# Modulation blocks in the even projection's weight stream: fewer among the attention's levels, more among the last blocks

## The chip, the cores and the metric

The kernel runs on one core of one Trainium2 chip. The metric is the device time of one execution in microseconds, lower is better. Before the change three runs gave 1708.02, 1708.63 and 1709.81 us, median 1708.63.

## What is computed

A two-layer hybrid block is followed by a second hybrid layer. Only the first mixer of the first block matters here. Two vectors of conditions (one for the context, one for the latents) are put through a silu and multiplied with a 1024 x 6144 matrix `mod_w` for each layer; the 48 groups of 128 results are shifts, scales and gates. The 512 tokens (256 context, 256 latent) are normalised and modulated with the first 16 groups. They are then projected, and the projected features feed a gated linear attention and an mLSTM:

```
def modulate(x, g, shift, scale):
    return rmsnorm(x, g) * (1 + scale) + shift

gq, gk, gv, gg, mq, mk, mv, mo, mg = _split(h @ w_in, EVEN_SIZES)
log_a = log_sigmoid((h @ a1[d]) @ a2[d] + ab[d]) / GLA_TAU
qk = silu(dwconv1d(concatenate([mq, mk]), conv_w, conv_b))
```

In `gla_scan` the scores need `exp(cum[t] - cum[s])` inside a chunk.

## The kernel before, in words

All weights lie in DRAM as blocks of 128 x 1024 floats (eight 128 x 128 tiles, 512 KB), in the order of the list `STREAM` (line 115). SP loads them one after another into a ring of four slots (`load_weights`, line 278). The load at place p of the stream waits until the block at place p - 4 is released, and since SP takes them in order, a load also waits for all loads ahead of it.

Two kinds of blocks share this stream in the even projection:

- 31 product blocks `even_in`. ScalarE (ACT) makes the rounded high part (line 375). For blocks 3 to 7 VectorE (DVE) makes the low part (line 385). From block 8 on ACT writes the negated high part (line 378), and a DMA of POOL adds the weights from DRAM to it (line 392). Such a block's slot is free when its high part is made. TensorE (PE) multiplies three passes (high by high, high by low, low by high).
- 28 modulation blocks `mod0` 16 to 43. DVE handles one with two multiply-and-accumulate instructions, one for each vector of conditions (line 865), and its slot is free after the second. Their sums are read in later stages.

`run_products` (line 402) writes every engine's program, item by item (item e is one 128-feature output of all tokens, or one tile of tokens; each is 24 passes of TensorE). Four banks hold the items. `low_parts` places the modulation blocks in DVE's order: before DVE goes past product block n it handles every modulation block that stands ahead of n in `STREAM`. At item e the bound is `due[e]`, here block e + 3. Within the last convolution (items 17 and 18) DVE is asked to go one block further, to block 22, between two taps:

```
ahead = parts_due(first + last_of[convs[-1]]) + AHEAD
...
if t == n_taps // 2 and group[-1] == len(convs) - 1:
    low_parts(ahead)
```

Items 0 to 4 are features (`low`, `gq`, `gk`), 5 to 8 token tiles (`gv`), 9 and 10 gates, 11 to 18 go through a convolution (two taps on DVE, line 706, in pairs of items), 19 to 22 are `mv`, 23 to 26 `gg`, 27 to 30 `mo`.

Beside the items runs `GlaSteps`, the gated linear attention, placed by half items ("ticks", two to an item). Its seven levels begin at tick 13 and are four ticks apart. For each level DVE subtracts sums (line 1832), ACT takes exponentials (line 1756), DVE takes the scores of the level before (line 1807) and makes four products (lines 1846 to 1849), and PE computes the scores (line 1634, 32 matmuls). So DVE's turn of the levels 5, 6 and 7 lies in items 14 and 15, 16 and 17, 18 and 19. After the levels come the keys (line 1870, items 22 and 23), the states (lines 1881 and 1884, items 24 to 26), and among them the mLSTM's gates: DVE sums and scans them in items 24 and 25 (lines 1950 to 1971), ACT makes `floors` (line 1975), and PE turns them (lines 1981 and 1982) in item 26, in front of that item's second half. The next round (`mo`) needs all four banks.

Each engine takes its instructions in the written order, so what DVE is given ahead of a level delays that level.

Of the kernel before, what the change touches and what calls it, by code (L numbers as in the profile page):

```python
# [56 lines left out]
TOGETHER = 3  # L57
# [22 lines left out]
def blocks_of(name):  # L80
    first = FIRST_TILE[name] // TPB
    return list(range(first, first + N_TILES[name] // TPB))
# [9 lines left out]
def spread_among(few, many):  # L92

    out, placed = [], 0
    for i, b in enumerate(many):
        while placed < len(few) * (i + 1) // len(many):
            out.append(few[placed])
            placed += 1
        out.append(b)
    return out  # L100


MOD_FIRST = 16
MOD_GROUP = 4
MOD_STRIP = 32
SQUARES_AT = 6
MOD_EVEN = 44
MOD_DOWN = 27
MOD_ODD = 42
DOWN_FIRST = 4  # L110
# [2 lines left out]
SSD_ENTERING = 4  # L113

STREAM = blocks_of("mod0")[:MOD_FIRST] + blocks_of("even_in")[:TOGETHER] \
    + spread_among(blocks_of("mod0")[MOD_FIRST:MOD_EVEN], blocks_of("even_in")[TOGETHER:]) \
    + blocks_of("even_out")[:TOGETHER] + spread_among(blocks_of("mod0")[MOD_EVEN:], blocks_of("even_out")[TOGETHER:]) \
    + blocks_of("up0") + blocks_of("down0")[:DOWN_FIRST] \
    + spread_among(blocks_of("mod1")[:MOD_DOWN], blocks_of("down0")[DOWN_FIRST:]) \
    + blocks_of("ssd_in")[:TOGETHER] + spread_among(blocks_of("mod1")[MOD_DOWN:MOD_ODD], blocks_of("ssd_in")[TOGETHER:MOD_SSD]) \  # L120
    + blocks_of("ssd_in")[MOD_SSD:]
# [237 lines left out]
def run_products(K, rounds, mods=None, prepare=None, beside=None, banks=BANKS, acc_slots=8, fill=0, tail=0):  # L359

    with K.scope():
        _run_products(K, rounds, mods, prepare, beside or Beside(), banks, acc_slots, fill, tail)
# [29 lines left out]
def first_together(rounds, n=TOGETHER):  # L396


    return [[it for r in rounds[:n] for it in r]] + rounds[n:]
# [1040 lines left out]
def even_mixer(K, f, gates, modulator):  # L1440

    ending = MlstmEnding(K, f, gates[2])
    with K.scope():
        mlstm(K, f, *gates, ending)

    with K.activations(KD * T):
        parts = ending.of([(f[name][:, j, :], *K.h_parts(T, base + j))
                           for name, base in (("gg", 0), ("mq", 4)) for j in range(4)])
        run_products(K, first_together(residual_items(K, "even_out", KD, lambda k: K.h_parts(T, k), 0,
                                                      lambda m, which: K.mod[:, 0, 16 + m, which:which + 1])),  # L1450
                     (modulator, blocks_of("mod0")[MOD_EVEN:]), prepare=parts, beside=SumSquares(K, 0), banks=BANKS - 1,
                     fill=8)
# [11 lines left out]
def even_projection(K, f, normalise, modulator, a2, gate_buffers):  # L1464
# [11 lines left out]
    def put(dest, func, scale=1.0, after=None):  # L1476
        def empty(act, bank):
            if after is not None:
                act.wait_ge(*after())
            return act.activation(dest, bank[0:dest.shape[0], :], func, scale=scale)  # L1480
        return empty
# [5 lines left out]
    def tokens(empty):  # L1487
        nonlocal tile
        groups = token_products(K, tile, T, range(TT), GW)
        rounds.append([Item(g, empty(i)) for i, g in enumerate(groups)])  # L1490
        tile += 4 * KD
# [25 lines left out]
    tokens(lambda i: put(f["mo"][:, i, :], ACT.Sigmoid, after=gla.outputs_made))  # L1517
    run_products(K, first_together(rounds), (modulator, blocks_of("mod0")[MOD_FIRST:MOD_EVEN]), normalise, gla, banks=4, acc_slots=4, fill=2, tail=12)

# [816 lines left out]
def odd_mixer(K, mods):  # L2336

    modulator, blocks = mods
    late = MOD_ODD - MOD_DOWN
    with K.scope():  # L2340
        zs, xl, xc = K.take(KI, LAT), K.take(KI, LAT), K.take(KI, CTX)
        bt, ct, dcol = K.take(SG, T), K.take(SG, LAT), K.take(4, 64)
        rows = K.take(LAT, dtype=F32R)
        xt, cb = K.take(2, LT, 512), K.take(2, 2, 3 * P)
        masks = K.take(32, dtype=F32R), K.take(P, dtype=BF16), K.take(2, 2, P, dtype=BF16)
        entering = K.take(SSD_ENTERING, 2, LAT)
        state = xc.rearrange("p (g i) t -> p g (i t)", g=SG).rearrange("p g (d x) -> p g d x", d=2)
        with K.activations(KD * T):
            ssd_projection(K, zs, xl, xc, bt, ct, dcol, rows, state, xt, cb, masks, entering, (modulator, blocks[:late]))
        with K.scope():  # L2350
            normed = ssd_latent(K, xl, zs, bt, ct, dcol, rows, state, xt, cb, masks, entering)
        with K.activations(KI * LAT):
            parts = Split(K, [(xl[:, c, :], *K.h_parts(LAT, c)) for c in range(KI)], normed, NORMED)
            run_products(K, residual_items(K, "ssd_out", KI, lambda k: K.h_parts(LAT, k), CTX,
                                           lambda m, which: K.mod[:, 1, 16 + m, which:which + 1]),
                         (modulator, blocks[late:]), prepare=parts,
                         beside=SumSquares(K, CTX), banks=BANKS - 1, fill=8)
# [1284 lines left out]
def build(nc, dram, out):  # L3642

    with ExitStack() as ctx:
        K = Kit(nc, ctx, dram)
        modulator = Modulator(K, K.take(2, D))
        with K.scope():
# [11 lines left out]
            even_mixer(K, f, gates, modulator)  # L3659
        feed_forward(K, 0, 0, (modulator, blocks_of("mod1")[:MOD_DOWN]))  # L3660
        odd_mixer(K, (modulator, blocks_of("mod1")[MOD_DOWN:]))
        K.late = K.take(LATE_COLS)
# [168 lines left out]
```

## Time and profile before

| what | us |
|---|---|
| median of three runs | 1708.63 |
| the profiled execution | 1706.59 |
| its span | 1704.2 |
| PE busy, share of the span | 1641.5, 96% |
| DVE busy | 1310.2, 77% |
| ACT busy | 906.8, 53% |
| mean granted clock of PE | 0.989 |

The profile is one execution. Its own time is 2.4 us above its span and 2.0 us below the median of the runs. "Busy" of PE counts pipelined matmuls, so a busy PE can still hide small gaps; a wait is seen in the bracket behind a row, with what ended it. The even projection lies between about 42 and 262 us of the span.

### The profile page before, as it was taken

How to read it: one execution, taken by the hardware profiler on the slowest of the kernel's cores; microseconds unless marked ns; L12 is line 12 of the kernel's file. 1: busy time of each engine (PE TensorE's matmuls, PEld its weight loads, DVE VectorE, ACT ScalarE, POOL GpSimd, SP SyncE). 2: the span in 40 equal slices, each digit the busy share in tenths (PEclk: the TensorE clock that was granted, in tenths of full speed). 3: DMA queues.
4: the chain of work that ended last, by engine and by line, in shares of the span. 5: the costliest groups of instructions: out<-in, count | busy, mean ns of one | idle time of the engine just before them, and what ended most of it. 6: DMA issues, size and time to landing. Idle time of an engine off the chain costs nothing. (4 is left out here: it accounts for less than half of the span.)

```text
span 1704.2 us, 26146 instructions
## 1 busy us (share of the span) xinstructions
PE 1641.5 (96%) x10046; PEld 1390.4 (82%) x10046; DVE 1310.2 (77%) x2483; ACT 906.8 (53%) x1558; POOL 53.7 (3%) x99
## 2 busy tenths in 40 slices
PE   5999999899999999999999999999999999999998
PEld 1787776778888888878888558899998988989997
DVE  3789856778999999969974788599965546765595
ACT  3756638555444432265554665455455567665541
POOL 0311100000000000000000000010000000000000
PEclk8999999999999999999999999999999999999999
DMA  8588850133323337734554326587665454444453
GB/s 321 200 223 208 242 153 1 51 135 99 99 99 99 99 113 251 240 113 143 183 173 124 100 75 212 176 210 223 190 193 183 150 169 147 137 124 127 146 161 112
DMA packets 75363, 264.35 MB, mean 155 GB/s; under 512 B 8591, under 2 KB 10312, under 8 KB 74856
## 3 DMA queue, kind: packets, MB, share of 16 engines
q1 hardware_dynamic: 67736, 240.47, 42.7%
q0 software_dynamic: 5424, 19.47, 6.4%
q10 hardware_dynamic: 2080, 2.76, 0.5%
q8 instruction: 79, 1.29, 0.3%
q14 instruction: 44, 0.36, 0.1%
HBM read 261.22 MB, written 1.18 MB: 154 GB/s over the span
## 5 line engine op out<-in xcount | busy, mean ns | idle before, releaser
L536 PE MATMUL banks<-m,weights_high 128*128 128x256 f32 (+1 forms) x4336 | 1018.7, 328 | 10.3 <-DVE weights_low L385 8.7
L536 PEld LDWEIGHTS banks<-m,weights_high 128*128 128x128 f32 x4336 | 729.0, 190 | 91.6 <-issue 11.6
L536 PE MATMUL banks<-m,weights_low 128*128 128x256 f32 (+1 forms) x2168 | 704.6, 325 | 0.0
L385 DVE TENSOR_TENSOR weights_low<-weight_ring,weights_high 128x1024 fp32r<-128x1024 f32 x270 | 326.7, 1221 | 170.0 <-ACT weights_high L375 169.0
L375 ACT ACTIVATE weights_high<-weight_ring 128x1024 fp32r<-128x1024 f32 x305 | 321.8, 1057 | 242.1 <-DMA weight_ring<-in_weights 153.0
L536 PEld LDWEIGHTS banks<-m,weights_low 128*128 128x128 f32 x2168 | 411.9, 190 | 34.5
L706 DVE SCALAR_TENSOR_TENSOR m<-m,columns 128x189 f32<-128x189 f32 (+4 forms) x504 | 199.2, 468 | 8.0 <-ACT m L643 7.8
L865 DVE SCALAR_TENSOR_TENSOR m<-weight_ring,m 128x1024 bf16<-128x1024 f32 x160 | 195.6, 1223 | 8.0 <-ACT m L844 2.5
L642 ACT ACTIVATE m<-banks,columns 128x512 f32<-128x512 f32 (+1 forms) x76 | 58.3, 767 | 144.9 <-PE banks L536 141.1
L706 DVE SCALAR_TENSOR_TENSOR m<-m 128x189 f32<-128x189 f32 (+2 forms) x352 | 122.8, 428 | 6.6 <-ACT m L643 6.6
L536 PE MATMUL banks<-m,weight_ring 128*128 128x256 f32 x512 | 112.6, 379 | 0.0
L536 PEld LDWEIGHTS banks<-m,weight_ring 128*128 128x128 f32 x512 | 96.3, 190 | 12.6
L536 PE MATMUL banks<-weights_high,m 128*128 128x512 f32 (+1 forms) x288 | 89.5, 388 | 2.9 <-ACT m L1480 2.7
L2896 ACT ACTIVATE m<-banks 128x256 f32<-128x256 f32 x74 | 28.6, 386 | 100.3 <-PE banks L536 96.2
L536 PEld LDWEIGHTS banks<-weights_high,m 128*128 128x128 f32 x288 | 54.0, 191 | 14.9 <-ACT m L1480 3.6
L643 ACT ACTIVATE m<-banks 128x512 f32<-128x512 f32 (+1 forms) x120 | 60.5, 504 | 0.0
L536 PE MATMUL banks<-weights_low,m 128*128 128x512 f32 (+1 forms) x144 | 55.2, 384 | 0.0
L642 ACT ACTIVATE m<-banks,columns,m 128x256 f32<-128x256 f32 x44 | 24.7, 561 | 42.3 <-PE banks L536 29.1
L392 POOL DMA_DIRECT2D weights_low<-in_weights x35 | 30.3, 865 | 438.7 <-ACT weights_low L378 438.7
L2741 DVE TENSOR_TENSOR m<-m 128x768 f32<-128x768 f32 x32 | 30.5, 952 | 11.4 <-ACT m L2810 11.4
L532 PE MATMUL banks<-m,weights_high 128*128 128x512 f32 (+1 forms) x96 | 35.6, 378 | 2.6 <-ACT m L981 2.5
L378 ACT ACTIVATE weights_low<-weights_high 128x1024 fp32r<-128x1024 f32 x35 | 37.1, 1060 | 1.1
(427 smaller groups left out, 1705.7 us busy)
## 6 DMA issues: line engine op xcount, KB each, us to landing
weight_ring<-in_weights SPq DMA_DIRECT2D x433, 512.0 KB, 4.2
weights_low<-in_weights POOLq DMA_DIRECT2D x35, 512.0 KB, 6.3
m<-entering SPq DMA_DIRECT2D x28, 256.0 KB, 3.0
x<-in_tokens SPq DMA_DIRECT2D x2, 1024.0 KB, 9.0
m<-in_cmp_w SPq DMA_DIRECT2D x1, 2048.0 KB, 7.2
m<-in_cond SPq DMA_DIRECT2D x2, 512.0 KB, 4.4
m<-entering POOLq DMA_DIRECT2D x4, 256.0 KB, 5.4
out<-x ACTq DMA_DIRECT2D x8, 128.0 KB, 1.9
```

The costliest lines, as they stand in the source:

```text
L375: act.activation(K.w_hi[:, g % PARTS, :], K.ring[:, place % RING, :], ACT.Copy).then_inc(*K.high_done.up())
L378: act.activation(K.w_lo[:, g % PARTS, :], K.w_hi[:, g % PARTS, :].bitcast(F32), ACT.Copy, scale=-1.0).then_inc(*K.minus_done.up())
L385: dve.tensor_tensor(K.w_lo[:, g % PARTS, :], K.ring[:, PLACE[PRODUCT_BLOCKS[g]] % RING, :], K.w_hi[:, g % PARTS, :].bitcast(F32), ALU.subt ...
L392: pool.dma_start(K.w_lo[:, g % PARTS, :], K.dram["weights"][PLACE[PRODUCT_BLOCKS[g]]], accum_op=ALU.add).then_inc(K.low_landed[g % PARTS]. ...
L532: pe.matmul(out, lhsT, rhs, start=p.start and i == 0, stop=False)
L536: mm = pe.matmul(out, lhsT, rhs, start=p.start and i == 0, stop=p.stop and i == len(passes) - 1)
L642: act.activation(acc[:, i % ACC, 0:c.n], bank[:, 0:c.n], ACT.Identity, bias=c.bias, scale=c.centre)
L643: act.activation(raw[:, i % RAW, 0:c.n], bank[:, 0:c.n], ACT.Copy).then_inc(*free_act.up())
L706: ins = dve.scalar_tensor_tensor(o, shift(raw[:, i % RAW, 0:c.n]), w, o, ALU.mult, ALU.add)
L865: dve.scalar_tensor_tensor(self.unread, K.ring[:, place % RING, :], 1.0, self.cond[:, c, :], ALU.mult, ALU.mult, accum_out=K.mod[:, layer, ...
L2741: dve.tensor_tensor(w, w, mid(cb[:, g % 2, d, :], 2), ALU.mult).then_inc(*weighted.up())
L2896: act.activation(dest, bank[:, 0:LAT], func_of[func], scale=scale))])
```

## The change

The 28 modulation blocks are no longer spread evenly among the 28 product blocks 3 to 30. Twelve (16 to 27) are spread among the product blocks 3 to 19, and sixteen (28 to 43) among the blocks 20 to 30.

```
+MOD_LEVELS, EVEN_LEVELS = 28, 20
...
-    + spread_among(blocks_of("mod0")[MOD_FIRST:MOD_EVEN], blocks_of("even_in")[TOGETHER:]) \
+    + spread_among(blocks_of("mod0")[MOD_FIRST:MOD_LEVELS], blocks_of("even_in")[TOGETHER:EVEN_LEVELS]) \
+    + spread_among(blocks_of("mod0")[MOD_LEVELS:MOD_EVEN], blocks_of("even_in")[EVEN_LEVELS:]) \
```

`STREAM` also sets how the weights are laid out in DRAM, so loads follow the new order. From place 75 of the stream on nothing differs. Written out, the number of modulation blocks that DVE handles at item e is:

```
item e   0 1 2 3 4 5 6 7 8 9 10 11 12 13 14 15 16 17 18 19 20 21 22 23 24 25 26 27
before   1 1 1 1 1 1 1 1 1 1 1  1  1  1  1  1  1  1  1  1  1  1  1  1  1  1  1  1
after    0 1 1 0 1 1 0 1 1 1 0  1  1  0  1  1  1  1  1  2  1  2  1  2  1  2  1  2
```

The blocks of item 19 are those that are taken between the taps of the last convolution.

## Rows read from the trace of the kernel before

**Rows 1.** Waits of PE between 40 and 260 us: in total, times, longest.
```profile
PE banks L1634 <- DVE m L1849: 3.8, 4, 1.3
PE banks L536 <- ACT m L1480: 2.7, 2, 1.9
```

**Rows 2.** Windows of 20 us: length, PE, PEld, DVE, ACT, POOL busy, PE clock, DMA.
```profile
160.00:180.00 20.00, 18.91 (x125) 15.50 (x123) 19.86 (x30) 12.54 (x18) 2.56 (x3) 1.00 0.88 215
```

**Rows 3.** Timeline of PE: start, length, line, [idle before <- releaser].
```profile
76.51 0.47 PE L536 MATMUL banks<-weights_high,m 128*128 128x512 f32 x1 [1.86 <-ACT m L1480]
...
144.97 2.06 PE L1634 MATMUL banks<-m 64*128 64x128 f32 x32 [0.32 <-DVE m L1849]
...
159.50 2.06 PE L1634 MATMUL banks<-m 64*128 64x128 f32 x32 [1.08 <-DVE m L1849]
...
188.56 2.06 PE L1634 MATMUL banks<-m 64*128 64x128 f32 x32 [1.27 <-DVE m L1849]
...
198.92 1.03 PE L1680 MATMUL banks<-m 128*128 128x256 f32 x4
...
229.16 0.25 PE L1981 MATMUL banks<-identity,m 36*128 36x36 f32 x1
...
233.74 0.47 PE L536 MATMUL banks<-weights_high,m 128*128 128x512 f32 x1 [0.89 <-ACT m L1480]
```

**Rows 4.** Timeline of DVE: the copy of the decays, item 3.
```profile
71.58 2.28 DVE L1811 TENSOR_SCALAR m<-banks 128x2048 f32<-128x2048 f32 x1
```

**Rows 5.** Timeline of ACT ahead of the levels, and at item 14.
```profile
73.89 1.88 ACT L1739 ACTIVATE m<-banks 128x2048 f32<-128x2048 f32 x1
75.67 0.59 ACT L1480 ACTIVATE m<-banks 128x512 f32<-128x512 f32 x1
...
145.37 0.59 ACT L643 ACTIVATE m<-banks 128x512 f32<-128x512 f32 x1
```

**Rows 6.** Timeline of DVE in and behind the levels.
```profile
147.15 2.73 DVE L706 SCALAR_TENSOR_TENSOR m<-m,columns 128x510 f32<-128x510 f32 x4
...
188.34 1.22 DVE L865 SCALAR_TENSOR_TENSOR m<-weight_ring,m 128x1024 bf16<-128x1024 f32 x1
...
193.38 2.48 DVE L1807 COPY_PREDICATED m<-m,banks 128x2048 f32<-128x2048 int32 x1
195.77 1.19 DVE L1858 TENSOR_TENSOR m<-m 128x1024 f32<-128x1024 f32 x1
...
202.35 1.28 DVE L1870 TENSOR_TENSOR m<-m,banks 128x512 f32<-128x512 f32 x2 [1.69 <-ACT m L1764]
...
210.07 1.29 DVE L1870 TENSOR_TENSOR m<-m,banks 128x512 f32<-128x512 f32 x2 [4.03 <-ACT m L1770]
...
215.72 0.89 DVE L1881 COPY m<-banks 128x128 f32<-128x128 f32 x4 [1.95 <-PE banks L1697]
...
241.47 1.28 DVE L1895 TENSOR_REDUCE m<-m 128x4 f32<-128x512 f32 x2 [6.45 <-ACT m L1781]
```

**Rows 7.** Timeline of ACT: the gates' floors, the emptying of item 26.
```profile
227.58 0.64 ACT L1975 ACTIVATE m<-m 36x512 f32<-36x512 f32 x1 [1.53 <-DVE m L1968]
...
232.88 0.60 ACT L1480 ACTIVATE m<-banks 128x512 f32<-128x512 f32 x1 [2.63 <-PE banks L536]
```

**Rows 8.** DMA issues between 180 and 240 us: count, KB each, median us to landing.
```profile
weight_ring<-in_weights SPq DMA_DIRECT2D x18, 512.0 KB, 6.3
```

**Rows 9.** Later waits of PE (timeline), and windows around them.
```profile
1240.02 0.76 PE L536 MATMUL banks<-m,weights_high 128*128 128x256 f32 x2 [3.26 <-DVE weights_low L385]
...
1299.40 0.39 PE L532 MATMUL banks<-m,weights_high 128*128 128x256 f32 x1 [1.87 <-ACT m L981]
...
1240.00:1243.00 3.00, 2.98 (x14) 3.00 (x15) 3.00 (x3) 1.46 (x2) 0.00 (x0) 0.50 0.61 187
1243.00:1246.00 3.00, 3.00 (x26) 3.00 (x26) 0.51 (x2) 1.06 (x1) 0.00 (x0) 0.94 0.94 322
1299.00:1303.00 4.00, 3.50 (x27) 3.30 (x28) 4.00 (x12) 2.79 (x7) 0.00 (x0) 1.00 0.95 398
```

## The prediction, written before the result was known

> **What bounds the kernel now.** I read the page first: PE is busy nearly all the span and everything else is not, so a gain can only come from PE's waits. I then asked for PE's waits in the even projection [rows 1]. The reader is to see how small they are: the score matmuls wait 3.8 us in four places for the products of a level on DVE, and the first pass of a token round waits twice for ACT to empty a bank, 2.7 us in all. The third view is the windows: in the levels DVE is full, 19.86 of 20 us, while PE is not [rows 2]. The fourth is the timeline of each engine, for the order of work. It shows one wait of 1.86 us at 76.51 us and four at the levels: 0.32 at 144.97, 1.08 at 159.50, a like one at the next level, and 1.27 at 188.56 [rows 3]. So the stage is PE's, but in its levels DVE sets the pace. From the convolution at 147.15 to the end of level 7 at 188.34 DVE never stops [rows 6]; behind that it waits again: 1.69, 4.03 and 1.95 us [rows 6].
>
> **What the change adds and removes.** No work is added or removed. 28 blocks remain, all loads and all passes too; five blocks move, from items 0, 3, 6, 10 and 13 to items 19, 21, 23, 25 and 27. A block costs DVE 2.5 us: two of them stand between 188.34 and 193.38, 5.04 us [rows 6].
>
> *Ahead of the levels.* Items 0 and 3 lose their blocks, 5.0 us of DVE's work ahead of the copy of the decays at 71.58 [rows 4]. ACT's absolute value at 73.89 follows this copy, and behind that stands the emptying of item 4 at 75.67 [rows 5], on which the wait of 1.86 hangs. PE finishes item 4 at 76.51 - 1.86 = 74.65. Where ACT is free and only waits for PE, PE still stands for 0.89 at such an emptying (at 233.74) [rows 3]. So of 1.86 us at most 1.0 can go, and for that the copy has to come 1.0 us earlier, a fifth of what DVE is spared. I take a gain of **1.0 us**. Bounds: 0 if the loads, not DVE, hold the copy; 1.0.
>
> *In the levels.* This is where the count by item matters and not the total. The blocks taken out of items 6 and 10 stand ahead of levels for which PE does not wait (its first such wait is at 144.97 [rows 3]); only that of item 13 bears on one. Without it DVE is at the convolution of items 13 and 14 about 2.5 us earlier, but this convolution needs ACT's copy of item 14, which ends at 145.37 + 0.59 = 145.96 [rows 5]. DVE started it at 147.15 [rows 6]. So only 1.2 us is gained there, the rest becomes idle time. Items 14 to 18 keep one block each, as before. Then item 19 has two, and they stand between the taps of the last convolution, ahead of level 7. The stretch of 188.34 - 147.15 = 41.2 us becomes 41.2 + 2.5 = 43.7. Level 7 is made at 145.96 + 43.7 = 189.66 instead of 188.34, 1.3 us later. PE's own pace from scores to scores is 159.50 - 1.08 - 144.97 = 13.45 us. With DVE 1.2 us earlier at the first of them and 1.3 later at the last, the four waits become about 0, 0.2, 1.1 and 3.8 us, 5.1 in all in place of 3.8. The net is **+1.3 us**. Bounds: if the doubled block were hidden, -3.8 (all four waits gone); if nothing of item 13 were gained, +2.5.
>
> *The clock after the long wait.* Later in this trace PE waits 3.26 us ahead of 1240.02, and the granted clock of the next 3 us is 0.50 (1.2 GHz): 14 matmuls in 3 us against 26 in the 3 us behind, so 3 x 12/26 = 1.4 us is lost. A wait of 1.87 us at 1299.40 left it at 1.00 [rows 9]. A wait of 3.8 us is nearer to the first. I take **+1.5 us**, an estimate from these rows; bounds 0 and 1.7 (half of 3.4, if the fall lasts somewhat longer). The Trainium skill, "TensorE: Matmul & The Clock Gate", section "HAM oscillation — how this bites in real kernels", says that waits of PE between bursts let the gate throttle it again, so that each burst starts cold. By that rule the 3.8 us wait costs the 1.5 us, and without it the sum is 1.5 us lower; it speaks against this change, and the row at 1240.02 agrees.
>
> *Behind the levels.* DVE's order is now: item 20 one block, 21 two, 22 one, 23 two, 24 one, 25 two, 26 one, 27 two. From the end of level 7 to the first states (215.72 - 188.34 = 27.4 us) there are two more blocks (items 21 and 23), 5.0 us, against the three waits of 1.69 + 4.03 + 1.95 = 7.7 us [rows 6]: they are covered. The tightest point within is the last taking of scores, made at 195.77, which PE wants at 198.92 [rows 3, 6]: a margin of 3.15 us for the 2.5 us of item 21. That leaves 0.6 us. If this cover were gone the cost would be what lies over it, at most 2.5 us.
>
> The second block of item 25 has less cover. It stands between the gates' sums and the states at which the scans follow. ACT's floors wait for these scans (idle for 1.53 us, start 227.58, end 228.22) [rows 7], and PE turns the floors at 229.16 without a wait [rows 3]. The cover is 229.16 - 228.22 = 0.9 us against 2.5. So PE waits **1.6 us** there, in the middle of item 26. ACT in turn is held at the floors, and behind them are the high part of block 29 and the emptying of item 26, on which the `mo` round hangs (its 0.89 us wait at 233.74 [rows 3]); ACT stands idle for 2.63 us ahead of this emptying, at 232.88 [rows 7], and PE's wait shifts the work that it waits for too, so the round moves with PE and no more. Bounds: 0 if DVE came early, 2.5 if there were no cover.
>
> The doubled blocks of item 27 stand ahead of a reduction for which DVE idles 6.45 us now [rows 6]. I cost them at nothing: item 27's own second block and the one of item 25 together are 5.0 us; without that cover they would cost these 5.0.
>
> *Loads.* Each load waits for the release four places ahead, and with two modulation blocks in a row this is DVE's more often. A load takes 6.3 us to land here [rows 8]. Product block 26 hangs on the block of item 22. DVE ends that one behind level 7 by four blocks (10.0 us), the taking of scores (195.77 - 193.38 = 2.4) and the two products with their copies (some 2.4, as long, an estimate): 14.8 us. It lands at 14.8 + 6.3 = 21.1. ACT makes its parts before the second keys' exponential, for which DVE stops waiting at 210.07 - 188.34 = 21.7 now [rows 6]. So the second keys come later by about what ACT needs for three instructions, some 3 us, of which the 1.95 us ahead of the states and the slack of the one block between cover most. I take 0 when PE itself is 1.5 us later through the clock, 0.8 otherwise; upper bound 2.
>
> **Sum.** -1.0 + 1.3 + 1.5 + 1.6 = +3.4 us. Nothing behind the stage changes, so it carries through to the end. Against the profiled execution, 1706.59, that is 1710.0; its time is 2.0 below the median, and 1708.63 + 3.4 = **1712.0 us**.
>
> **The rivals.**
>
> *A, no fall of the clock.* The wait falls so that the clock stays at 1.00, as at 1299.40. Then -1.0 + 1.3 + 1.6 + 0.4 (half of the loads' 0.8) = +2.3 us, 1710.9.
>
> *B, the relief works (other side).* One mechanism: DVE catches up ahead of level 7, so that the doubled block of item 19 is free. PE wants level 7 at 144.65 + 3 x 13.45 = 185.0, DVE can start at 145.96, so the 43.7 us would have to be 39.0; the point is 4.7 us of slack that the rows do not show, since DVE is full there [rows 2]. Then the four waits vanish: -3.8 - 1.0 = -4.8 us, 1703.8. For it: DVE has fewer blocks in all by item 18. Against it: four of the five that move are taken from items where PE does not wait for DVE's levels.
>
> *C, more behind the levels.* The 1.6 us wait at the floors, with the 0.89 us wait 3 us behind it, brings the clock down a second time, +1.5, and the loads add up to 1: about +5.5 us, 1714.1. For it: these are two waits close together. Against it: 1.87 us alone did nothing at 1299.40.
>
> *D, nothing to be measured.* The floors' wait is covered, and the clock stays up: -1.0 + 1.3 = +0.3, 1708.9. For it: only 1.6 us and the clock separate it from the forecast.
>
> **How the numbers follow.** Chances: the forecast 0.42, A 0.22, B 0.10, C 0.14, D 0.12. A kernel of this kind is told from no change by about 0.2%, 3.4 us, so the limits are 1705.2 and 1712.0. The forecast sits on the upper one, and I put half of it on either side. Slower: 0.22 of the forecast's 0.42, 0.14 of C and 0.04 of A make 0.40. Faster: 0.10 from B, less what would end inside the limit, and some from other ways to gain, 0.11. The same: 0.49. The range of 8 in 10 goes from 1706.5 (D with luck at the loads) to 1715.0 (C and a little); it leaves B out. The forecast's own range is 1710.5 to 1714.
>
> **What would show each step right.** In the profile after: the wait at 76.5 us shrinks to about 0.9 and the time is some 75.5. DVE shows idle time ahead of the convolution near 145. Three level waits near 0, 0.2 and 1.1 us, then one of 3 to 4 us ahead of the scores near 189, and the granted clock at 0.50 behind it. PE waits about 1.6 us for ACT's floors near 233. Wrong would be: a wait ahead of level 7 under 1.5 us, for then DVE was not bound as I read it; or PE waiting for a bank near 204 us or for weights in items 24 to 26, for then the loads decide.

## The result, and the profile after

The changed kernel takes 1711.83 us (median of 11 runs, 1708.77 to 1716.20), the kernel before in the same series 1708.02 (11 runs, 1704.64 to 1710.77). The ratio is 1.0026, 95% interval 1.0015 to 1.0037. So it is slower by 0.26%. The medians alone differ by 3.8 us, 0.22%; the ratio is formed from all runs. The forecast was +3.4 us, 1712.0. The profiled execution of the changed kernel took 1711.64 us, its span is 1709.9.

In the changed kernel's file the lines below the edit stand two further down: the score matmuls are L1636, the products of a level L1851, ACT's emptying L1482, a modulation block L867.

The waits of PE from 60 to 265 us (total, times, longest), where the two views of before are [rows 1] and [rows 3]:

```profile
PE banks L1636 <- DVE m L1851: 5.3, 3, 3.9
PE banks L538 <- ACT m L1482: 1.8, 2, 0.9
PE banks L1983 <- ACT m L1977: 1.7, 1, 1.7
```

The timeline of PE after, only the rows that bear a wait, and the first pass for the keys (201.73):

```profile
76.32 0.47 PE L538 MATMUL banks<-weights_high,m 128*128 128x512 f32 x1 [0.89 <-ACT m L1482]
...
158.14 2.06 PE L1636 MATMUL banks<-m 64*128 64x128 f32 x32 [0.31 <-DVE m L1851]
...
172.68 2.06 PE L1636 MATMUL banks<-m 64*128 64x128 f32 x32 [1.09 <-DVE m L1851]
...
189.82 3.12 PE L1636 MATMUL banks<-m 64*128 64x128 f32 x32 [3.89 <-DVE m L1851]
...
201.73 1.02 PE L1682 MATMUL banks<-m 128*128 128x256 f32 x4
...
233.71 0.25 PE L1983 MATMUL banks<-identity,m 36*128 36x36 f32 x1 [1.67 <-ACT m L1977]
...
239.83 0.47 PE L538 MATMUL banks<-weights_high,m 128*128 128x512 f32 x1 [0.89 <-ACT m L1482]
```

Read it against [rows 3]. The wait at 76 us went from 1.86 to 0.89. The wait ahead of level 4 is gone, levels 5 and 6 wait 0.31 and 1.09, and level 7 waits 3.89 in place of 1.27. Behind it the 32 score matmuls take 3.12 us in place of 2.06: the same work at a lower clock. The wait of 1.67 us for ACT's floors is new.

DVE in the same stretch shows why. The convolution of items 13 and 14 now waits for ACT, and the last convolution has two modulation blocks (four lines L867 with 1024 elements) between its two halves:

```profile
145.78 2.73 DVE L708 SCALAR_TENSOR_TENSOR m<-m,columns 128x510 f32<-128x510 f32 x4 [1.16 <-ACT m L645]
...
174.86 1.41 DVE L708 SCALAR_TENSOR_TENSOR m<-m,columns 128x510 f32<-128x510 f32 x2
176.19 1.22 DVE L867 SCALAR_TENSOR_TENSOR m<-weight_ring,m 128x1024 bf16<-128x1024 f32 x1
...
177.44 1.23 DVE L867 SCALAR_TENSOR_TENSOR m<-weight_ring,m 128x1024 bf16<-128x1024 f32 x1
...
178.82 1.23 DVE L867 SCALAR_TENSOR_TENSOR m<-weight_ring,m 128x1024 bf16<-128x1024 f32 x1
...
180.09 1.23 DVE L867 SCALAR_TENSOR_TENSOR m<-weight_ring,m 128x1024 bf16<-128x1024 f32 x1
...
181.24 1.41 DVE L708 SCALAR_TENSOR_TENSOR m<-m,columns 128x510 f32<-128x510 f32 x2
...
189.59 1.22 DVE L867 SCALAR_TENSOR_TENSOR m<-weight_ring,m 128x1024 bf16<-128x1024 f32 x1
```

From 145.78 to 189.59 DVE has 43.8 us without a pause, where the kernel before had 41.2 [rows 6].

The windows tell of the clock (behind the length stand the five busy times, then PEclk; 0.50 is 1.2 GHz, 1.00 is 2.4 GHz, and a value between is a window with both). PE did nothing from 186 to 189; behind this wait, and again behind the one at the floors, part of the stretch runs at half clock:

```profile
186.00:189.00 3.00, 0.00 (x0) 0.00 (x0) 3.00 (x5) 2.97 (x5) 0.00 (x0) 1.00 0.97 208
189.00:192.00 3.00, 2.18 (x26) 2.21 (x28) 2.96 (x5) 2.61 (x3) 0.87 (x1) 0.76 0.29 30
192.00:195.00 3.00, 3.00 (x17) 2.42 (x15) 2.70 (x7) 0.00 (x0) 0.00 (x0) 0.67 1.03 244
...
234.00:238.00 4.00, 4.00 (x17) 3.20 (x16) 3.95 (x10) 1.66 (x2) 0.86 (x1) 0.62 0.19 18
```

The stretch adds up. From the first pass at 76 us to the first pass of the `mo` round it is 239.83 - 76.32 = 163.51 us after and 233.74 - 76.51 = 157.23 before [rows 3]: +6.28. Of that the level waits are 5.29 - 3.76 = +1.53. Scores of level 7 to first keys is 201.73 - 189.82 = 11.91 in place of 198.92 - 188.56 = 10.36: +1.55, the clock. The floors' wait is +1.67. From there to the `mo` round it is 6.12 in place of 4.58: +1.54, the clock a second time. Together 6.29.

The wait that ends at 76 us is 0.97 shorter, so the terms come to +5.3 us. Little of this gain is seen in the times of this pair: the pass begins 0.19 us earlier and not 0.97, since what lies ahead of it took longer here. Its start varies from execution to execution, 74.83 to 77.60 us in the kernels below that have the same short wait. Behind the stretch nothing changes: from the first pass of the `mo` round to the end of the span it is 1709.9 - 239.83 = 1470.1 us after and 1704.2 - 233.74 = 1470.5 before. The spans differ by 5.7, the two profiled executions by 1711.64 - 1706.59 = 5.05, the medians by 3.8. One pair does not tell how many of the other executions are like it.

### The profile page after: what moved, and what is told of

Its sections match the earlier page's. It is cut to its first block and busy times, and to the rows that moved or that the text cites. A ratio compares the mean times of both kernels' runs of the same rounds, so it can differ in the third digit from the quotient of the medians.

```text
span 1709.9 us, 26146 instructions
## 1 busy us (share of the span) xinstructions
PE 1644.9 (96%) x10046; PEld 1393.7 (82%) x10046; DVE 1311.5 (77%) x2483; ACT 907.6 (53%) x1558; POOL 53.6 (3%) x99
## 5 line engine op out<-in xcount | busy, mean ns | idle before, releaser
L867 DVE SCALAR_TENSOR_TENSOR m<-weight_ring,m 128x1024 bf16<-128x1024 f32 x160 | 195.6, 1223 | 6.1 <-DMA weight_ring<-in_weights 1.0
```

The costliest lines, as they stand in the source:

```text
L867: dve.scalar_tensor_tensor(self.unread, K.ring[:, place % RING, :], 1.0, self.cond[:, c, :], ALU.mult, ALU.mult, accum_out=K.mod[:, layer, ...
```

## The experiments

All of them change only how many modulation blocks stand ahead of each product block. In place of the calls of `spread_among` the list is made from counts by item:

```
+EVEN_COUNTS = [...]                      # one number for each of the items 0 to 27
+
+def placed_by_counts(few, many, counts):
+    out, few = [], list(few)
+    for n, b in zip(counts, many):
+        out += few[:n]
+        few = few[n:]
+        out.append(b)
+    assert not few
+    return out
...
-    + spread_among(blocks_of("mod0")[MOD_FIRST:MOD_LEVELS], blocks_of("even_in")[TOGETHER:EVEN_LEVELS]) \
-    + spread_among(blocks_of("mod0")[MOD_LEVELS:MOD_EVEN], blocks_of("even_in")[EVEN_LEVELS:]) \
+    + placed_by_counts(blocks_of("mod0")[MOD_FIRST:MOD_EVEN], blocks_of("even_in")[TOGETHER:], EVEN_COUNTS) \
```

In these files the lines stand another twelve down (scores L1648, products of a level L1863, emptying L1494, keys' products L1884, floors L1989). No kernel leaves out any work. Times are medians of the kernel's runs; the ratio, with its 95% interval, is formed from all runs, those of the kernel before on the same chip beside it, and can differ a little from the ratio of the medians.

**The doubled block ahead of level 7, undone.** From the changed kernel:

```
-item 19: 2, item 27: 2
+item 19: 1, item 27: 3
```

> The changed kernel, but item 19 has one modulation block and item 27 three. Theory 1 (the doubled block ahead of level 7 costs): the stretch is 2.5 us shorter, the wait ahead of level 7 falls from 3.9 to about 1.3 us, the granted clock stays at 1.00 behind it, and the wait of 1.7 us at the floors stays. That is 2.6 + 1.5 = 4.1 us under the changed kernel where that one had a fall of the clock: ratio to the kernel before about 1.000 (0.999 to 1.001). Theory 2 (the loads, sixteen modulation blocks among eleven product blocks): still sixteen among these, so the ratio stays at about 1.0026.

Measured: 1709.90 us, ratio 1.0009 (0.9994 to 1.0023). Its timeline of PE:

```profile
188.49 2.06 PE L1648 MATMUL banks<-m 64*128 64x128 f32 x32 [1.26 <-DVE m L1863]
...
215.37 1.09 PE L1711 MATMUL banks<-m 128*64 128x128 f32 x16 [0.87 <-DVE m L1884]
...
232.82 0.32 PE L1995 MATMUL banks<-identity,m 36*128 36x36 f32 x1 [2.72 <-ACT m L1989]
...
240.19 0.47 PE L550 MATMUL banks<-weights_high,m 128*128 128x512 f32 x1 [0.89 <-ACT m L1494]
```

The level's wait is 1.26 and its matmuls are back at 2.06 us, as theory 1 has it, and the interval leaves out the 1.0026 of theory 2, if narrowly. But two things came that I had not written down: a wait of 0.87 for the second keys, and 2.72 at the floors in place of 1.67. ACT shows where they come from. It stands 4.44 us for a load, makes the two parts, and only then takes the keys' exponentials:

```profile
210.94 1.06 ACT L389 ACTIVATE weights_high<-weight_ring 128x1024 fp32r<-128x1024 f32 x1 [4.44 <-DMA weight_ring<-in_weights]
212.03 1.06 ACT L392 ACTIVATE weights_low<-weights_high 128x1024 fp32r<-128x1024 f32 x1
212.99 1.00 ACT L1784 ACTIVATE m<-banks 128x1024 f32<-128x1024 f32 x1
```

So theory 2, the loads, has a part in it: once PE is not held up ahead of it, the late block costs 0.87 + (2.72 - 1.67) = 1.9 us. The clock fell at the floors too: from row to row it is 240.19 - 232.82 = 7.37 us in place of 4.58, so this fall cost 2.79 us, more than the two of the changed kernel (1.55 and 1.54).

**The doubled block ahead of the floors, undone.** From the changed kernel:

```
-item 25: 2, item 27: 2
+item 25: 1, item 27: 3
```

> The changed kernel, but item 25 has one modulation block and item 27 three. Theory 1: the wait of 1.7 us at the floors is gone, and with it the second fall of the clock behind it (1.5 us where it comes); the wait of 3.9 us ahead of level 7 stays. Ratio to the kernel before about 1.001 (1.0005 to 1.002). Theory 2 (the loads): no wait of PE changes by more than 0.5 us, 1.0026.

Measured: 1709.46 us, ratio 1.0006 (0.9993 to 1.0019). The floors' wait is gone, that of level 7 stays, and its matmuls are slow:

```profile
189.28 3.63 PE L1648 MATMUL banks<-m 64*128 64x128 f32 x32 [3.88 <-DVE m L1863]
...
236.03 0.47 PE L550 MATMUL banks<-weights_high,m 128*128 128x512 f32 x1 [0.89 <-ACT m L1494]
```

Theory 1 holds, and the interval leaves out the 1.0026 of theory 2.

**Both undone.**

```
-item 19: 2, item 25: 2, item 26: 1, item 27: 2
+item 19: 1, item 25: 1, item 26: 2, item 27: 3
```

> The changed kernel with one block in item 19 and in item 25, two in item 26 and three in item 27. Theory 1: waits of 0.3, 1.1 and 1.3 us at levels 5 to 7, none at the floors, 0.9 us at 76 us; against the kernel before -1.0 (the early wait) - 1.1 (the levels) = -2.1 us, ratio 0.9988 (0.998 to 0.9995). Theory 2 (the loads): the second stretch is as crowded as in the changed kernel, so 1.001 or more.

Measured: 1707.29 us, ratio 0.9995 (0.9981 to 1.0008). The interval holds both the 0.9988 written down and 1, so no gain is shown by it; theory 2's 1.001 is left out, narrowly. In its profile the waits are those written down: 0.89 at 75 us, 0.30, 1.09 and 1.27 at the levels, none for the keys and none at the floors. Items 21 and 23 are double here too, and the load is late as well, only less:

```profile
207.89 1.06 ACT L389 ACTIVATE weights_high<-weight_ring 128x1024 fp32r<-128x1024 f32 x1 [3.62 <-DMA weight_ring<-in_weights]
...
226.46 0.63 ACT L1989 ACTIVATE m<-m 36x512 f32<-36x512 f32 x1 [2.59 <-DVE m L1982]
```

From DVE's last read of item 22's block (its accumulator read, which ends at 200.99) to the high part of block 26 it is 6.9 us here, and 7.7 (203.23 to 210.94) in the first experiment, where PE waited 0.87 for the keys. Up to there both kernels have the same order, so the difference is that of two executions. The floors end at 226.46 + 0.63 = 227.09 and PE turns them at 227.14: the 0.94 us of cover of the kernel before [rows 3, 7] are used up, though no wait is seen. This is why item 25's second block costs 2.72 us behind a late load and 1.67 without one.

**One doubling alone, in the kernel before: item 19.**

```
-item 19: 1, item 27: 1
+item 19: 2, item 27: 0
```

> The kernel before with one edit: item 19 has two modulation blocks and item 27 none. Theory 1: level 7 is made 2.5 us later, the wait ahead of it rises from 1.3 to 3.8 us, and the granted clock falls to 0.50 behind it in most runs (1.5 us more): +2.5 to +4.0 us, ratio 1.0015 to 1.0024. Rival (the doubled block is hidden, DVE has slack in item 19): 1.000.

Measured: 1712.55 us, ratio 1.0019 (1.0006 to 1.0032). One block moved by eight items makes the kernel 0.2% slower. The waits at the levels are 0.32, 1.11, 1.08 and then 3.87. The wait at 77 us is 2.73 here and 1.68 in the next kernel, 1.86 in the kernel before, and all three have the same order up to there; this wait varies by itself while the blocks of items 0 and 3 are in place:

```profile
77.25 0.47 PE L550 MATMUL banks<-weights_high,m 128*128 128x512 f32 x1 [2.73 <-ACT m L1494]
...
191.93 3.69 PE L1648 MATMUL banks<-m 64*128 64x128 f32 x32 [3.87 <-DVE m L1863]
```

**One doubling alone, in the kernel before: item 25.**

```
-item 25: 1, item 27: 1
+item 25: 2, item 27: 0
```

> The kernel before with one edit: item 25 has two modulation blocks and item 27 none. Theory 1: the floors come 2.5 us later, PE waits 1.6 us for them in item 26, no fall of the clock in most runs: +1.6 us, ratio 1.0009 (1.0003 to 1.002). Rival (covered, since PE's other work stands there): 1.000 and no such wait.

Measured: 1711.14 us, ratio 1.0015 (1.0003 to 1.0026). The level waits are those of before, and PE waits at the floors:

```profile
231.04 0.25 PE L1995 MATMUL banks<-identity,m 36*128 36x36 f32 x1 [1.67 <-ACT m L1989]
...
235.61 0.47 PE L550 MATMUL banks<-weights_high,m 128*128 128x512 f32 x1 [0.89 <-ACT m L1494]
```

In this profile the clock did not fall (4.57 us from row to row, as before).

**The early part alone.** From the kernel before:

```
-item 0: 1, item 3: 1, item 26: 1, item 27: 1
+item 0: 0, item 3: 0, item 26: 2, item 27: 2
```

> The kernel before with the blocks of items 0 and 3 moved to items 26 and 27. Theory 1: the wait for ACT's emptying at 76 us falls from 1.9 to 0.9 us, the four level waits stay at 3.8 us in all, nothing else: -1.0 us, ratio 0.9994 (0.999 to 1.000). Rival (the loads hold the copy of the decays): the wait stays at 1.9 us.

Measured: 1705.69 us, ratio 0.9991 (0.9979 to 1.0002). The interval reaches 1, so the time shows no gain, but the profile has the wait at 0.89 and the levels unchanged (0.31, 1.09, 1.08, 1.28):

```profile
77.41 0.47 PE L550 MATMUL banks<-weights_high,m 128*128 128x512 f32 x1 [0.89 <-ACT m L1494]
```

**Relief of the levels themselves.** From the kernel before, all counts 1 but these:

```
+items 0, 3, 13, 16 and 18: 0
+items 21, 23 and 26: 2, item 27: 3
```

> The kernel before with the blocks of items 0, 3, 13, 16 and 18 taken out and one more in items 21, 23 and 26 and two more in item 27 (three). Theory 1 (a level's pace is DVE's two blocks): with one block less in each of levels 4, 6 and 7, PE waits at most 0.3 us in the levels instead of 3.8, 0.9 instead of 1.9 at 76 us, and nothing at the floors: -3.5 - 1.0 = -4.5 us, ratio 0.9974 (0.9965 to 0.9985). Rival (more blocks behind the levels cannot be hidden there): as many blocks follow item 19 as in the changed kernel but one, so a ratio of 1.000 or more.

Measured: 1702.62 us, ratio 0.9970 (0.9957 to 0.9983), faster than both kernels. PE waits 0.30 and 0.47 us at the levels, somewhat more than expected, and 0.54 for the keys (items 21 and 23 are double, the late load again; item 25 is single here):

```profile
157.24 2.06 PE L1648 MATMUL banks<-m 64*128 64x128 f32 x32 [0.30 <-DVE m L1863]
...
184.38 2.06 PE L1648 MATMUL banks<-m 64*128 64x128 f32 x32 [0.47 <-DVE m L1863]
...
210.91 1.09 PE L1711 MATMUL banks<-m 128*64 128x128 f32 x16 [0.54 <-DVE m L1884]
```

It has 14 blocks up to item 18, as many as the changed kernel, and the same 14 from item 19 on; the kernel before has 19 and 9. One of the two kernels with 14 is 0.3% faster and the other 0.26% slower, so it is the places that count and not the total.

**Into DVE's gaps ahead of the levels.**

```
+items 0, 3, 13, 15, 16 and 18: 0
+items 5, 11, 26 and 27: 2, item 6: 3
```

> The kernel before with the blocks of items 0, 3, 13, 15, 16 and 18 taken out; one more stands in items 5, 11, 26 and 27 and two more in item 6, where DVE idles in the trace of the changed kernel (4.6 us behind item 5, 8.7 us in item 6, 4.9 us ahead of the first convolution pair). Theory 1 (a block costs what of it lies over DVE's idle time at its item): no wait of PE at the levels, 0.9 us at 76 us, none for the keys since items 21 and 23 are single: -3.8 - 1.0 = -4.8 us, ratio 0.9972, and at or below the run with the blocks of items 0, 3, 13, 16 and 18 moved behind the levels. Rival (what counts is how few blocks stand ahead of item 19, as the changed kernel has it): 25 stand there instead of 14 or 19, so PE waits at the levels as before, 1.000.

Measured: 1702.65 us, ratio 0.9975 (0.9962 to 0.9988). The expectation miscounts: 17 blocks stand ahead of item 19, not 25 (24 ahead of item 26). That is three more than in the changed kernel, and it is as fast as the last one; the rival is out. No wait for the keys is left, and one of 0.30 us at level 6, but a new one stands ahead of level 1, 1.10 us. Its cause is a load again, as ACT shows:

```profile
97.40 1.06 ACT L389 ACTIVATE weights_high<-weight_ring 128x1024 fp32r<-128x1024 f32 x1 [3.15 <-DMA weight_ring<-in_weights]
98.50 1.06 ACT L392 ACTIVATE weights_low<-weights_high 128x1024 fp32r<-128x1024 f32 x1
```

**The late load, by itself.** From the changed kernel, with item 25 left double:

```
-item 19: 2, item 21: 2, item 23: 2, item 26: 1, item 27: 2
+item 19: 1, item 21: 1, item 23: 1, item 26: 2, item 27: 4
```

> The changed kernel with one block in items 19, 21 and 23, two in items 25 and 26, and four in item 27. It tells the waits of the run with a single block in item 19 apart (0.87 us for the keys, 2.72 us at the floors). Theory 1 with the loads (block 26 comes late through the doubled blocks of items 21 and 23, and makes the second keys late): the wait for the keys is gone, and the wait at the floors is back at 1.6 to 1.7 us. Rival (the floors' wait of 2.72 us comes from item 25's double alone): it stays at 2.7 us.

Measured: 1708.01 us, ratio 1.0005 (0.9991 to 1.0020). The waits of the first experiment come apart as the loads have it: none for the keys, and the floors' is back:

```profile
228.27 0.25 PE L1995 MATMUL banks<-identity,m 36*128 36x36 f32 x1 [1.67 <-ACT m L1989]
...
234.15 0.47 PE L550 MATMUL banks<-weights_high,m 128*128 128x512 f32 x1 [0.89 <-ACT m L1494]
```

From row to row it is 5.88 us in place of 4.58, so here the clock fell behind the same wait of 1.67 us behind which it did not fall with item 25 doubled alone.

**No item with three ahead of the levels.**

```
+items 0, 3, 13, 15, 16 and 18: 0
+items 5, 6, 10, 12, 26 and 27: 2
```

> As the run with the blocks of items 0, 3, 13, 15, 16 and 18 taken out, but no item has three: two each in items 5, 6, 10, 12, 26 and 27. Theory (the wait of 1.10 us ahead of level 1 in that run came from item 6's third block, through the late load of product block 10 and ACT's work behind it): that wait is gone, the levels' waits are at most 0.3 us in all, ratio to the kernel before 0.9970 (0.996 to 0.998). Rival (any doubling ahead of level 1 costs): the wait of 1.1 us stays.

Measured: 1704.19 us (6 runs, on another chip than the other experiments), ratio 0.9966 (0.9953 to 0.9978). The wait ahead of level 1 is gone, though items 5 and 6 are still double, so it was the third block of item 6. What is left at the levels is 0.55 us in all, where 0.3 was expected:

```profile
143.19 2.06 PE L1648 MATMUL banks<-m 64*128 64x128 f32 x32 [0.23 <-DVE m L1863]
...
170.34 2.06 PE L1648 MATMUL banks<-m 64*128 64x128 f32 x32 [0.32 <-DVE m L1863]
```

Its interval overlaps those of the two other fast kernels (0.9970 and 0.9975); the three can't be ranked by time.

## Why the prediction was right, step by step

*Ahead of the levels, -1.0.* The wait is 0.97 shorter in the profile (1.86 to 0.89). It is 0.89 in all nine profiles in which items 0 and 3 have no block, and 1.68, 1.86 and 2.73 in the three in which they have one, so 1.0 lies in what is gained, 0.8 to 1.8. Right in kind; the start of the pass, forecast at 75.5, was 76.32.

*In the levels, +1.3.* Measured +1.53. The waits forecast as 0, 0.2, 1.1 and 3.8 are 0, 0.31, 1.09 and 3.89. The steps held one by one: the convolution of items 13 and 14 waits for ACT, so of the 2.5 us of item 13's block 1.16 are lost as idle time and the convolution starts 1.37 earlier, and the stretch behind it is 43.8 us (43.7 forecast). One doubling alone brings the wait to 3.87, its undoing to 1.26. This is shown.

*The clock, +1.5.* Measured 1.55, 1.57 and 1.62 us in the three profiles with a wait of 3.9 us (scores to keys 11.91, 11.93 and 11.98 in place of 10.36), and 0 in the five with a wait of 1.25 to 1.28 (10.35 or 10.36). Right in size and in kind at level 7. The upper bound of 1.7 rests on a fall of 3.4 us, and no row shows such a length; behind the floors the falls cost 1.54 and 1.30, and 2.79 in the first experiment, over that bound.

*The floors, +1.6.* Measured 1.67, in three kernels, and 2.72 in the first experiment, where the late load had used up the cover. Right.

*The cover behind the levels.* No wait of PE at the first keys; DVE ended the last taking of scores at 199.7, two us ahead of PE at 201.7, more than the 0.6 us forecast because the fallen clock holds PE back. Without the fall, in the first experiment, it is 198.34 against 198.85, 0.5 us. Right.

*The loads, 0 with the fall of the clock and 0.8 without.* In the changed kernel nothing. Without the fall of the clock it varied: 1.9 us in the first experiment, in two waits, near the upper bound of 2, but 0.54 with the levels relieved and none with both doublings undone. What was missing in the working is that the delay is paid a second time at the floors, where it uses up the cover of 0.9 us that item 25's second block was counted against.

*Item 27, nothing.* DVE still idles 4.46 us ahead of the reduction (6.45 before), so the doubled block there is covered. Right.

*The sum.* The forecast was +3.4; the medians give +3.8. The profiled pair gives +5.3, because in it the clock fell twice. That is the mechanism of rival C without its part for the loads, 3.4 + 1.5 = +4.9. (C's +5.5 is added up wrongly: with 1.0 for the loads its terms make +5.9.) So in the one execution of the changed kernel that was looked at, the forecast left out a term of 1.5 us, the second fall, and that the median still came within 0.4 us of it is luck as far as the runs show. In the four profiles with a wait at the floors the clock fell behind it three times (1.67, 1.67 and 2.72 us) and once not (1.67). Which share of the timed runs has it is open; I did not measure the clock of the stretch in them. The spread of the changed kernel's runs, 7.4 us, is no proof of it, for the kernel before spreads by 6.1. The absolute 1712.0 against 1711.83 looks closer than it is, since the kernel before measured 1708.02 in this series and not the 1708.63 that the forecast started from. Rival B, the relief that was to be had, asked for 4.7 us less on DVE in the levels; the change gives 2.5 more at the end of them instead. In the changed kernel B did not happen. With one block out of each of the levels 4, 6 and 7 the gain that it priced is there: 0.9970, -5.1 us, where B gave -4.8.

The chances (slower 0.40, the same 0.49) were more cautious than the working: it gave +3.4 us and the limit was 3.4. The most likely outcome by these chances, the same, is not what came; the measured 0.26% lies just beyond the limit of 0.2%.

## What to carry to other kernels

Work that is moved out of a busy stretch helps only where it stands on the chain that someone waits for: count it item by item against the idle time of its engine there, not in total. Look at the last item of the stretch too, since a new density can begin one item early through a look-ahead (here, block 22 is taken in the last convolution). And where buffers are released by that work, two or three in a row can make a later load late, which is paid at the next point without cover.

## What the runs showed of the hardware that was not expected

A wait of PE of 1.67 us was followed by the lower clock in two profiles and not in a third, although all three waits stand at the same place of the program, and a wait of 1.87 us elsewhere left the clock up [rows 9]. So the length of the wait alone does not tell, and neither does its place; what decides is open. Nor is the price of a fall fixed: 1.30 to 2.79 us in six of them. And PE's wait for ACT's emptying ahead of the `mo` round is 0.89 us in all 12 profiles, though ACT stood idle ahead of it; no shorter wait of this kind was seen here.
